# The MLP of a hybrid RWKV-7/S5 step on one core: weights loaded in the stage before, layers interleaved, final norm folded in

## The reference

```python
h = rms_norm(x, norm2_g) * (1 + sc2) + sh2
x = x + g2 * (square(relu(h @ w_ff1)) @ w_ff2)     # w_ff1 1024 x 4096, w_ff2 4096 x 1024
y = rms_norm(x, norm_f_g)
```

## Time and profile before

| engine | busy us | share of the span |
|---|---|---|
| PE | 1850.5 | 78% |
| PEld | 1151.0 | 48% |
| DVE | 1025.3 | 43% |
| ACT | 630.7 | 27% |
| POOL | 526.0 | 22% |

### The profile page before, as it was taken

The page is one execution under the profiler, slowest core; times in us unless marked ns, Lnnn a source line. Parts: engine busy times, 40 slices in busy tenths (PEclk is TensorE's granted clock), DMA queues, the critical chain, the costliest instruction groups (busy, mean ns, idle before and its releaser), DMA issues. The chain is left out here.

```text
span 2378.0 us, 55997 instructions
## 1 busy us (share of the span) xinstructions
PE 1850.5 (78%) x24105; PEld 1151.0 (48%) x24160; DVE 1025.3 (43%) x1697; ACT 630.7 (27%) x1201; POOL 526.0 (22%) x579
## 2 busy tenths in 40 slices
PE   7935667548999478999983694899999999999970
PEld 1123367425555268888882342444545455454530
DVE  7964455540687634555553542122221222222224
ACT  0050134332445333444441223202111120110201
POOL 0032000033111044555552523121111121111101
PEclk9957679879999689999997797999999999999985
DMA  7861133102344433333335122211010011100014
GB/s 250 319 230 56 69 121 113 52 0 67 95 149 145 136 82 97 99 103 98 103 92 199 72 94 101 71 36 71 35 35 35 35 38 68 35 35 0 0 44 141
DMA packets 168129, 215.37 MB, mean 91 GB/s; under 512 B 36822, under 2 KB 122838, under 8 KB 166234
## 3 DMA queue, kind: packets, MB, share of 16 engines
q1 hardware_dynamic: 162396, 201.07, 26.0%
q10 hardware_dynamic: 4352, 8.39, 1.0%
q0 software_dynamic: 1296, 4.72, 0.5%
HBM read 151.63 MB, written 60.42 MB: 89 GB/s over the span
## 5 line engine op out<-in xcount | busy, mean ns | idle before, releaser
L89 PE MATMUL psum<-arena 128*128 128x384 bf16 (+1 forms) x2006 | 708.5, 353 | 118.4 <-POOL arena L986 30.1
L90 PE MATMUL psum<-arena 128*128 128x384 bf16 (+1 forms) x2019 | 714.9, 354 | 81.1 <-DVE arena L2205 44.8
L91 PE MATMUL psum<-arena 128*128 128x384 bf16 (+2 forms) x2004 | 708.1, 353 | 0.5
L89 PEld LDWEIGHTS psum<-arena 128*128 128x128 bf16 (+1 forms) x2028 | 202.4, 100 | 392.0 <-issue 58.3
L1561 PE MATMUL psum<-arena 64*64 64x64 f32 x9216 | 345.5, 223 | 34.2 <-issue 27.2
L1561 PEld LDWEIGHTS psum<-arena 64*64 64x64 f32 x9216 | 310.3, 135 | 50.3 <-issue 45.2
L1555 PE MATMUL psum<-arena 64*64 64x64 f32 (+2 forms) x6336 | 284.8, 238 | 55.0 <-DMA arena<-xrec 39.1
L91 PEld LDWEIGHTS psum<-arena 128*128 128x128 bf16 (+1 forms) x2028 | 202.9, 100 | 183.5 <-issue 17.2
L90 PEld LDWEIGHTS psum<-arena 128*128 128x128 bf16 (+1 forms) x2028 | 202.6, 100 | 176.1 <-issue 13.5
L1555 PEld LDWEIGHTS psum<-arena 64*64 64x64 f32 x6336 | 244.1, 135 | 63.6 <-issue 60.9
L1688 ACT ACTIVATE arena<-psum 128x192 f32<-128x192 f32 (+2 forms) x624 | 173.0, 334 | 286.3 <-PE psum L1561 183.4
(11 more groups left out here) (273 smaller groups left out, 1967.6 us busy)
## 6 DMA issues: line engine op xcount, KB each, us to landing
arena<-in_w_ff SPq DMA_DIRECT2D x16, 2048.0 KB, 7.9
arena<-in_w_ada SPq DMA_DIRECT2D x12, 2048.0 KB, 9.7
arena<-xrec SPq DMA_DIRECT2D x72, 320.0 KB, 3.4
arena<-s_tab SPq DMA_DIRECT2D x8, 1600.0 KB, 7.3
x<-arena SPq DMA_DIRECT2D x18, 512.0 KB, 3.0
xrec<-arena SPq DMA_DIRECT2D x4, 2304.0 KB
arena<-xrec SPq DMA_DIRECT2D x72, 128.0 KB
arena<-x SPq DMA_DIRECT2D x18, 512.0 KB, 3.8
```

The lines of the kernel that those rows point to most:

```text
L89: nc.tensor.matmul(out, whi, xhi, start=first, stop=False)
L90: nc.tensor.matmul(out, wlo, xhi, start=False, stop=False)
L91: return nc.tensor.matmul(out, whi, xlo, start=False, stop=last)
```

## The change

The MLP is written anew, and `stage_last` goes into it.

- In close, SP loads the first 2 MB of w_ff1 behind the gate rows. ScalarE splits a quarter of it (128x1024) after each scaled copy of blocks 2 to 5, GpSimd makes the remainders after those of blocks 3 to 6. Both first wait until the memory that the parts go to is no longer read in close.
- In the MLP the loops over rounds are written out. The order on TensorE is first layer 0, then for j = 1 to 7 first layer j and second layer j-1, then second layer 7. `hhi` and `hlo` have two buffers.
- The split of w1 for round j+1 is done in four pieces, each after the copy of the tile of round j whose weights it overwrites.
- w2 of the last round is split into the memory of w1, after the last first layer.
- The accumulator isn't cleared; round 0 copies into it. In the last first layer's round DVE, after accumulating a block, multiplies it with the gate and adds x (`base`). The second layer of round 7 uses all eight banks in pairs, and DVE finishes each block from PSUM: times gate, plus base, then the norm's scale (`total`, `leave`). SP stores y.
- The MLP's semaphores are cleared at the end of the program; the last stage, which cleared none, is gone.

The diff, cut to its core:

```diff
 # stage_close, sync
             sp.dma_start(gate, ins["gates"][0].partition_broadcast(P)).then_inc(ev("gate_rows"), 16)
+            sp.dma_start(M.w1s, ins["w_ff1"][:, :, 0:512]).then_inc(ev("w1"), 16)
 # stage_close, scalar, after the scaled copy of block b
+                if 2 <= b < 6:
+                    cols = slice((b - 2) * P, (b - 1) * P)
+                    act.wait_ge(ev("w1"), 16)
+                    act.wait_ge(ev("out"), NCT)
+                    nc.scalar.activation(M.w1hi[:, :, cols], M.w1s[:, :, cols], ACT.Copy).then_inc(ev("w1_hi"), 1)
 # stage_close, gpsimd, after the remainder of block b-1
+                if 3 <= b < 7:
+                    cols = slice((b - 3) * P, (b - 2) * P)
+                    pool.wait_ge(ev("gate"), NCT)
+                    pool.wait_ge(ev("w1_hi"), b - 2)
+                    nc.gpsimd.tensor_tensor(M.w1lo[:, :, cols], M.w1s[:, :, cols], M.w1hi[:, :, cols], ALU.subtract).then_inc(ev("w1_lo"), 1)
 # stage_mlp, tensor
+            first(0)
+            for j in range(1, ROUNDS):
+                first(j)
+                second(j - 1)
+            pe.wait_ge(ev("relu"), ROUNDS * O)
+            second(LAST)
 # stage_mlp, sync
+            load1(1)
+            load2(0)
+            for j in range(1, ROUNDS):
+                sp.wait_ge(ev("w1_lo"), O * j)
+                if j + 1 < ROUNDS:
+                    load1(j + 1)
+                else:
...                 gate rows, x of blocks 0 and 1
+                sp.wait_ge(ev("w2_lo"), j)
+                load2(j)
 # stage_mlp, scalar
+            def split2(j):
+                act.wait_ge(ev("w2"), 16 * j + 16)
+                if j == LAST:
+                    act.wait_ge(ev("ff1"), ROUNDS * O)
+                else:
+                    need(act, ev("ff2"), 2 * NB * j)
+                nc.scalar.activation(w2(j)[0], w2s, ACT.Copy).then_inc(ev("w2_hi"), 1)
...                 for each tile of round j: relu, copy, then
+                    if j < LAST:
+                        split1(j + 1, o)
+                split2(j)
 # stage_mlp, vector, round j, after square and remainder of its four tiles
+                if j:
+                    for b in range(NB):
+                        for h in range(2):
+                            accumulate(j - 1, b, h)
+                        if j == LAST:
+                            base(b)
...
+            dve.wait_ge(ev("gf"), 16)
+            for b in range(NB):
+                total(b)
+                if b:
+                    leave(b - 1)
+            leave(NB - 1)
+            def base(b):
...
+                tt(a, a, gate[:, w], ALU.mult).then_inc(ev("gated"), 1)
+                dve.wait_ge(ev("gated"), b + 1)
+                dve.wait_ge(ev("x", b % 2), 16 * (b // 2) + 16)
+                tt(a, a, xt[b % 2], ALU.add).then_inc(ev("based"), 1)
 # program: the places of the first weights in the arena
+    M.w1s = M.arena.t[:, 47104:51200].rearrange("p (k n) -> p k n", k=KD)
+    M.w1hi = M.arena.t[:, 44288:46336].bitcast(BF16).rearrange("p (k n) -> p k n", k=KD)
+    M.w1lo = M.arena.t[:, 15619:17667].bitcast(BF16).rearrange("p (k n) -> p k n", k=KD)
```

More of the change, by code:

```diff
@@ L2127, in stage_close, with stage_mlp @@
     A.at = keep
-def stage_mlp(nc, M, ins):
+def stage_mlp(nc, M, ins, outs):
     A, ps = M.arena, M.ps
+    keep = A.at
     FW = 512
     ROUNDS, O = FF // FW, FW // P
-    M.acc = A.take(NB, D)
-    keep = A.at
-    w1s = A.take(KD, FW)
+    LAST = ROUNDS - 1
     w2s = A.take(O, D)
-    w1hi, w1lo = A.take(KD, FW, dt=BF16), A.take(KD, FW, dt=BF16)
+    w1s, w1hi, w1lo = M.w1s, M.w1hi, M.w1lo
+    A.at = 17667
+    acc = A.take(NB, D)
+    at_w2 = A.at
     w2hi, w2lo = A.take(O, D, dt=BF16), A.take(O, D, dt=BF16)
-    f = [A.take(T) for _ in range(2)]
-    hhi, hlo = A.take(O, T, dt=BF16), A.take(O, T, dt=BF16)
+    after_w2 = A.at
+    A.at = at_w2
+    gf = A.take(D)
+    z = [A.take(D) for _ in range(3)]
+    A.at = after_w2
+    flat = lambda v: v.rearrange("p k n -> p (k n)").rearrange("p (o n) -> p o n", o=O)
+    w2 = lambda j: (flat(w1hi), flat(w1lo)) if j == LAST else (w2hi, w2lo)
+    f = [A.take(T) for _ in range(2)]
+    hhi, hlo = ([A.take(O, T, dt=BF16) for _ in range(2)] for _ in range(2))
+    ss, ms, rs = ([A.take(1) for _ in range(2)] for _ in range(3))
+    free = w1s.rearrange("p k n -> p (k n)")
+    gate = free[:, 0:2 * D].rearrange("p (w n) -> p w n", w=2)
+    xt = [free[:, (2 + n) * D:(3 + n) * D] for n in range(2)]
+    two = lambda v: v.rearrange("p (h c) -> p h c", h=2)
     with ExitStack() as ctx:
@@ L2163, in _, with low2 @@
         def _(pool):
[L2164 to L2167, removed]
+            def low2(j):
+                hi, lo = w2(j)
                 pool.wait_ge(ev("w2_hi"), j + 1)
-                nc.gpsimd.tensor_tensor(w2lo, w2s, w2hi, ALU.subtract).then_inc(ev("w2_lo"), 1)
+                nc.gpsimd.tensor_tensor(lo, w2s, hi, ALU.subtract).then_inc(ev("w2_lo"), 1)
@@ L2193, in _, with split1 @@
[L2193 to L2211, removed]
+            def split1(j, o):
+                cols = slice(o * P, (o + 1) * P)
+                act.wait_ge(ev("w1"), 16 * j)
+                act.wait_ge(ev("ff1"), O * (j - 1) + o + 1)
+                nc.scalar.activation(w1hi[:, :, cols], w1s[:, :, cols], ACT.Copy).then_inc(ev("w1_hi"), 1)
@@ new lines, in split2 @@
+            def split2(j):
[5 more added lines that the diff above has]
+                nc.scalar.activation(w2(j)[0], w2s, ACT.Copy).then_inc(ev("w2_hi"), 1)
+            for j in range(ROUNDS):
+                for o in range(O):
+                    n = j * O + o
+                    act.wait_ge(ev("ff1"), n + 1)
+                    need(act, ev("h_lo"), n - 1)
+                    nc.scalar.activation(f[n % 2].rearrange("p (g c) -> p g c", g=TG), wide(ps, 3 * (n % 2)), ACT.Relu).then_inc(ev("relu"), 1)
+                    act.wait_ge(ev("square"), n + 1)
+                    if o == 0 and j >= 2:
+                        act.wait_ge(ev("ff2"), 2 * NB * (j - 1))
+                    nc.scalar.activation(hhi[j % 2][:, o], f[n % 2], ACT.Copy).then_inc(ev("h_hi"), 1)
+                    if j < LAST:
+                        split1(j + 1, o)
+                split2(j)
@@ L2213, in _, with first @@
+            for b in range(NB):
+                act.wait_ge(ev("sum"), b + 1)
+                need(act, ev("rstd"), b - 1)
+                nc.scalar.activation(w2s.rearrange("p o n -> p (o n)")[:, 0:D], z[b % 3], ACT.Square, accum_out=ss[b % 2]).then_inc(ev("squares"), 1)
+                act.wait_ge(ev("squares"), b + 1)
+                nc.scalar.activation(ms[b % 2], ss[b % 2], ACT.Copy, scale=1.0 / D, bias=RMS_EPS).then_inc(ev("mean_sq"), 1)
         @block.tensor
         def _(pe):
-            with pe.Fori(0, ROUNDS) as j:
-                pe.wait_ge(ev("w1_lo"), j + 1)
+            def first(j):
@@ L2226, in _, with second @@
                     last.then_inc(ev("ff1"), 1)
+            def second(j):
+                hi, lo = w2(j)
                 pe.wait_ge(ev("w2_lo"), j + 1)
@@ L2239, in _ @@
                         last.then_inc(ev("ff2"), 1)
[L2240 to L2285, removed]
@@ new lines, in total @@
+            def total(b):
+                w, v, bank = int(b == LB), z[b % 3], (0, 2, 4, 6)[b % 4]
+                dve.wait_ge(ev("ff2"), 2 * NB * LAST + 2 * b + 2)
+                need(dve, ev("y_out", b % 3), 16 * (b // 3))
+                tt(two(v), ps[:, bank:bank + 2, :], two(gate[:, w]), ALU.mult).then_inc(ev("final_read"), 1)
+                dve.wait_ge(ev("final_read"), b + 1)
+                dve.wait_ge(ev("based"), b + 1)
+                tt(v, v, acc[:, b], ALU.add).then_inc(ev("sum"), 1)
@@ new lines, in leave @@
+            def leave(b):
+                v = z[b % 3]
+                dve.wait_ge(ev("rstd"), b + 1)
+                dve.wait_ge(ev("sum"), b + 1)
+                nc.vector.scalar_tensor_tensor(out=v, in0=v, scalar=rs[b % 2], in1=gf, op0=ALU.mult, op1=ALU.mult).then_inc(ev("y"), 1)
+            for j in range(ROUNDS):
+                for o in range(O):
+                    n = j * O + o
+                    dve.wait_ge(ev("relu"), n + 1)
+                    tt(f[n % 2], f[n % 2], f[n % 2], ALU.mult).then_inc(ev("square"), 1)
+                    dve.wait_ge(ev("h_hi"), n + 1)
+                    tt(hlo[j % 2][:, o], f[n % 2], hhi[j % 2][:, o], ALU.subtract).then_inc(ev("h_lo"), 1)
+                if j:
+                    for b in range(NB):
+                        for h in range(2):
+                            accumulate(j - 1, b, h)
+                        if j == LAST:
+                            base(b)
@@ L2310, in stage_last @@
+            dve.wait_ge(ev("gf"), 16)
+            for b in range(NB):
+                total(b)
+                if b:
+                    leave(b - 1)
+            leave(NB - 1)
+    clear(nc, ev)
     A.at = keep
```

108 lines of the change are left out of this document (53 added, 55 removed).

## The result

| | median, us | runs | ratio to before | profiled execution (span) |
|---|---|---|---|---|
| before | 2382.93 (2376.85 to 2386.89) | 4 | 1 | 2379.68 (2378.0) |
| changed | 2250.76 (2247.90 to 2259.48) | 4 | 0.9454 [0.9419, 0.9488] | 2259.48 (2257.7) |

A forecast was written before the change was run, and what follows sets the result against it. TensorE was taken as the MLP's bound, with its idle time to be won: start -19.5, rounds -47, end -63.4, together -130 us. From the profiled run 2250, from the median 2256, so 2253 us; range with rivals 2236 to 2276.

The forecast's parts named there:

- A, start of the MLP: MLP's opening: first weights loaded and split during close, so TensorE starts with the block; 19.5 us less.
- close stage: Early load and four split pieces in close: cost put at 0, bounds 0 and 4 us.
- MLP's work and first tile: TensorE in the MLP: eight rounds at full clock 748.2 us, plus 2.9 for the slower first column tile.
- seven short waits: Second layers in seven rounds: TensorE waits 0.77 us each for DVE's first accumulate, 5.4 us, without a clock fall.
- the hold and its restart: Last round: GpSimd's split holds DVE's add, so TensorE stands 6.5 us, plus 2.0 restart; 8.5 us.
- last slot to the end: After the last matmul: event, multiply and add, norm and store, final clear; 13.0 us against 76.4.
- the second rival: MLP rounds: the clock falls at each of the seven short waits, 7 x 2.0 us; 2267 us, chance 10%.
- The first rival: Last round: DVE's add is not held or GpSimd comes late, so no stall; 2244 us, chance 14%.
- the clearing of the MLP's semaphores: Program's end: 28 semaphores cleared in 2.5 us; if nothing of it is measured, 2.5 us more gain.
- The base: Starting time for the whole sum: profiled run gives 2250, median 2256; 2253 us set between, blaming scatter on eight restarts.

The follow-up runs named there:

- E1: Changed kernel, but the first w1 is loaded and split inside the MLP's block, as before; 2265.04 us, 0.9518 of before.
- E7: E5, with the first block of each round's second layer (but the last) accumulating in PSUM banks 0 and 1; 2234.22 us, 0.9397 of before.
- E5: Changed kernel, but in the last round VectorE does the base of block b three blocks later; 2238.25 us, 0.9420 of before.
- E6: Changed kernel, but GpSimd's last remainder of the second-layer weights is replaced by two fills that read nothing; 2242.05 us, 0.9432 of before.

## Why the prediction was right

| step | forecast, us | measured, us | by |
|---|---|---|---|
| A, start of the MLP | -19.5 | -19.5 | seam 23.34 to 3.87; E1 19.8 |
| close stage | 0 (0 to 4) | 0.0 behind the square | 101.55 and 101.56 |
| MLP's work and first tile | 748.2 + 2.9 | 751.2 | 765.05 less the two rows below |
| seven short waits | 5.4 | 5.4 | E7 against E5 |
| the hold and its restart | 8.5 (6.5 + 2.0) | 8.4 (5.7 + 2.7) | E5 |
| last slot to the end | 13.0 | 11.4 | 2246.34 to 2257.7 |
| all | -130 | -131.6 | from the square |

- **The start.** 3.83 us of clearing instead of 3.61 was forecast from three more semaphores at some 0.07 us, and it came out so. ScalarE's pieces lie in idle time, as said: the square of the next block waits 5.66 us where it waited 6.60, and starts no later, 32.81 us behind the first one against 32.80.
- **The rounds.** The clock did not fall at the short waits, which the earlier trace rows had shown; this removes the second rival: the granted clock is 1.00 behind each of the seven. Its opposite is in the same trace: behind the 5.55 us wait TensorE ran at a granted clock of 0.74 in the 8 us shown. The 2.9 us of the first tile are 0.2 less than the two numbers that stand beside them give (14.8 and 11.7); the measured sum, 751.2 against 751.1, does not tell which is better.
- **The hold.** The chosen value, between 1 and 8.5, was the upper one, because the earlier trace rows showed a hold to the end of the other's instruction. That carried over from 2.4 us to 7.6. Its two halves were each off, by -0.8 and +0.7, and cancelled; that 8.4 stands beside 8.5 is luck. The standing is shorter because GpSimd's subtraction began 0.35 us before the multiply ended, not behind it, and took 7.63 us instead of 8.0. The restart was taken as the mean of the eight of before, 2.0, and this one cost 2.7. The first rival (no hold) is out in the changed kernel and was made true in E5 and E6.
- **The end.** The term that was mis-sized most is the clearing of the MLP's semaphores behind the last store, 2.5 forecast. From the last square to the end it is 8.65 us (2249.05 to 2257.7) where it was 7.8, so only 0.85 more. The rows under this list split it. The last store landed at 2376.7 before, 1.3 us ahead of the end, and at 2255.0 in the changed kernel, 2.7 ahead of it: what lies behind the store, now with the clearing, is 1.4 longer. From the square to that landing it is 0.6 less, with a store that goes through SyncE instead of GpSimd.
- **The base.** 2253 was set between two sums, 2250 and 2256, on the guess that the scatter of before came from the eight restarts. The runs don't bear this out: with one such restart left the changed kernel's four runs lie 11.6 us apart, before's 10.0, and the profiled executions scatter by 17 us ahead of the square, where no restart of the MLP has come yet. That the forecast lies 2 us from the median is in part luck; the sum itself, 130 against 131.6, is not.
- **Not foreseen, and free:** in round 1 VectorE's square of h (L2344) began while GpSimd's 7.99 us subtraction ran, and took 4.58 us instead of 1.36. The prediction had GpSimd done 1 us ahead of that square; but this subtraction is the first round's, whose ScalarE split comes behind all of that round's weight pieces and not at a buffer's release. TensorE did not wait, for the chain behind the square had a whole tile of 11.7 us.

The last store's issue in before (that of the changed kernel is shown above), and its size and time from issue to landing, before and after:

```profile
2373.84 0.58 POOL L2272 DMA_DIRECT2D out_y<-arena  x1 [1.62 <-DVE arena L2301]
...
out_y<-arena POOLq DMA_DIRECT2D x1, 512.0 KB, 2.9
...
out_y<-arena SPq DMA_DIRECT2D x1, 512.0 KB, 2.6
```

Most of the sum was not a matter of estimate: the work of TensorE is a count times a pace that before already showed, and with TensorE without a break the rest is the few places where it stands.

## What to carry to other kernels

Where one engine is the bound in a stage, count its work times its pace at full clock, and account for every microsecond above that: here waits, restarts behind them, one seam and one tail. Each of these was put back or taken out by an experiment, and moved the time by what it showed, to within 1 us. When work is moved onto VectorE, look at what GpSimd does at that very moment: an add with two SBUF inputs beside a GpSimd subtraction of 7.63 us took 8.34 us instead of 1.23, and moving the add by three blocks cost nothing. A wait's price is from matmul start to matmul start, 0.77 us for one that is listed as 0.61, and here the restart came on top only behind the long ones, of 5.6 us.

## What the runs showed of the hardware that had not been expected

- Clearing semaphores between two stages is no small change: the block that cleared 46 of them held the next stage up for 3.53 us, and the same instructions beside other work cost nothing that shows inside the span.
- GpSimd's fills of 128x4096 took 3.51 us each, for float32 and for bfloat16 alike, beside VectorE instructions that kept their 1.22 to 1.23 us.
- 0.6 us of standing left TensorE's granted clock at 1.00, as 1.00 us did in the earlier trace rows; behind 5.55 us it was at the lower level. No wait between 1.00 and 5.55 us is shown here.
